# One-hot rows of a retrieval layer, built per token instead of per eight tokens

## The reference

```python
def _peer(h, w_query, sub_keys, expert_u, expert_v):
    ...                      # for each token and each of 8 heads: 16 picks
    eid = i1 * N_KEYS + i2   # i1, i2 in 0..127; 16384 experts
    g = jax.nn.softmax(best_s, axis=-1)
    ...
    a = jax.nn.gelu(jnp.einsum('td,thkd->thk', hx, expert_u[e]))
    return jnp.einsum('thk,thkd->td', gw * a, expert_v[e])
```

## Time and profile before

| | us |
|---|---|
| median of 3 runs | 1741.33 |
| profiled execution, its own time | 1739.58 |
| its span, first to last instruction | 1737.5 |
| PE busy | 1523.0 |
| DVE busy | 1347.0 |
| POOL busy | 967.2 |
| ACT busy | 384.0 |

### The profile page before, as it was taken

One profiled execution on the slowest core, in us unless ns is written; L12 is line 12 of the kernel. 1 busy time (PEld: TensorE's weight loads), 2 busy tenths in 40 slices (PEclk: granted clock), 3 DMA queues, 4 the chain that ended last, 5 costly groups with the idle time before them and its releaser, 6 DMA issues.

```text
span 1737.5 us, 17042 instructions
## 1 busy us (share of the span) xinstructions
PE 1523.0 (88%) x6242; PEld 949.3 (55%) x6242; DVE 1347.0 (78%) x1915; ACT 384.0 (22%) x834; POOL 967.2 (56%) x591
## 2 busy tenths in 40 slices
PE   9999999999979915888788887899989899999976
PEld 8988999988668802333233333445535544444432
DVE  6666656666797999767768888888868998788787
ACT  5665455564201212011010101020210101000000
POOL 3210000000364677887786776788888478788661
PEclk9999999999989957999999998999999889999998
DMA  9876443466799999999999999999999899999996
GB/s 322 286 258 218 121 146 122 139 203 241 273 382 419 379 425 425 411 425 426 425 424 424 417 422 419 422 414 423 424 420 426 346 380 411 410 404 406 425 427 273
DMA packets 159380, 615.39 MB, mean 354 GB/s; under 512 B 20915, under 2 KB 74255, under 8 KB 96703
## 3 DMA queue, kind: packets, MB, share of 16 engines
q0 software_dynamic: 79232, 485.32, 68.1%
q1 hardware_dynamic: 80064, 128.99, 20.7%
HBM read 683.42 MB, written 2.10 MB: 395 GB/s over the span
## 4 chain that ended last, share of the span: by engine, by line
PE 29%; POOL 21%; DMA 18%; DVE 16%; issue 13%; DVEq 2%; ACT 1%; SPq 0%; POOLq 0%; ACTq 0%
PE psum_all L592 13%; DMA v_slot<-in_expert_v_dram,eid 12%; POOL v_slot L547 11%; POOL u_slot L528 9%; DVE u_slot L1793 8%; DMA u_slot<-in_expert_u_dram,eid 5%; PE psum_all L732 4%; PE psum_all L987 3%; DVE xh L1828 2%; PE psum_all L757 1%; PE psum_all L713 1%; PE psum_all L619 1%; PE psum_all L617 1%; POOL v_slot L550 1%; DMA wq_ring<-in_w_query_dram 0%
## 5 line engine op out<-in xcount | busy, mean ns | idle before, releaser
L1793 DVE SCALAR_TENSOR_TENSOR u_slot<-u_slot,xh 128x2048 f32<-128x2048 f32 x256 | 577.8, 2289 | 130.2 <-DMA u_slot<-in_expert_u_dram,eid 128.5
L987 PE MATMUL psum_all<-v_slot,diag 128*128 128x512 f32 x1152 | 556.1, 635 | 138.8 <-DMA v_slot<-in_expert_v_dram,eid 93.4
L528 POOL DMA_INDIRECT u_slot<-in_expert_u_dram,eid x256 | 452.6, 1768 | 290.1 <-DVE u_slot L1793 117.5
L547 POOL DMA_INDIRECT v_slot<-in_expert_v_dram,eid x224 | 420.8, 1879 | 92.7 <-issue 64.6
L987 PEld LDWEIGHTS psum_all<-v_slot,diag 128*128 128x128 f32 x1152 | 223.8, 201 | 448.2 <-issue 249.5
L1828 DVE SCALAR_TENSOR_TENSOR xh<-v_slot,gate,xh 128x2048 f32<-128x2048 f32 x100 | 235.2, 2352 | 52.2 <-DMA v_slot<-in_expert_v_dram,eid 45.4
L1411 DVE TENSOR_TENSOR w_lo<-w_ring,w_hi 128x512 fp32r<-128x512 f32 x240 | 156.8, 689 | 78.8 <-ACT w_hi L1036 75.6
L592 PE MATMUL psum_all<-act_hi,w_hi 128*128 128x256 f32 x640 | 184.6, 289 | 1.1 <-DVE w_lo L1411 1.0
L592 PE MATMUL psum_all<-act_hi,w_lo 128*128 128x256 f32 x640 | 180.7, 282 | 0.0
L592 PE MATMUL psum_all<-act_lo,w_hi 128*128 128x256 f32 x640 | 180.6, 282 | 0.0
L1036 ACT ACTIVATE w_hi<-w_ring 128x512 fp32r<-128x512 f32 x240 | 139.4, 622 | 42.8 <-PE psum_all L592 40.8
(11 more groups left out here) (293 smaller groups left out, 1608.4 us busy)
## 6 DMA issues: line engine op xcount, KB each, us to landing
w_ring<-in_w_in_dram SPq DMA_DIRECT2D x88, 512.0 KB, 4.8
u_slot<-in_expert_v_dram SPq DMA_DIRECT2D x40, 1024.0 KB, 8.9
wo_ring<-in_w_out_dram SPq DMA_DIRECT2D x32, 512.0 KB, 4.9
wq_ring<-in_w_query_dram SPq DMA_DIRECT2D x32, 512.0 KB, 10.1
w_ring<-in_cmp_k_w_dram POOLq DMA_DIRECT2D x16, 512.0 KB, 5.5
w_ring<-in_cmp_v_w_dram POOLq DMA_DIRECT2D x16, 512.0 KB, 4.3
u_slot<-in_expert_u_dram,eid POOLq DMA_INDIRECT x256
v_slot<-in_expert_v_dram,eid POOLq DMA_INDIRECT x256
```

Of the source, the lines that this page charges most:

```text
L528: nc.gpsimd.indirect_dma_start(out=u_slot[m % RU][:, :], out_offset=None, in_=expert_u[0], in_offset=bass.IndirectOffsetOnAxis(ap=eid[:, n ...
L547: nc.gpsimd.indirect_dma_start(out=v_slot[m % RV][:, :], out_offset=None, in_=expert_v[0], in_offset=src, bounds_check=ROWS - 1, oob_is_er ...
L987: ins = nc.tensor.matmul(bank[(4 if n < PH else 0) + q][:, :], diag[:, n % 2, k, :], v_slot[m % RV][:, 512 * q:512 * q + 512], start=(m in ...
L1793: V.scalar_tensor_tensor(u_slot[m % RU][:, :], u_slot[m % RU][:, :], 1.0, xh[:, n // PH, :], ALU.mult, ALU.mult, accum_out=u_dot[:, n, k:k ...
```

## The change

In `hot_rows` three operations on all eight tokens become two for each token. The comparison of the second key, 128 columns, takes the key as a per-partition scalar. The comparison of the first key, 40 columns, takes the key and the coefficient as two per-partition scalars, with the comparison and the product in one operation. The drain between goes, and the semaphore is raised by the last operation as before.

```diff
         def hot_rows(t, b):
 
             g, n = NG_T * t + b, PICKS[t]
-            cols = slice(G_TOK * b, G_TOK * b + G_TOK)
             if b == 0:
                 dve.wait_ge(S["pick_ok"], t + 1)
             if g >= 2:
                 dve.wait_ge(S["dense_mm"], g - 1)
-            row, key, coef = (pickT[0:n, t, i, cols].unsqueeze(2) for i in range(3))
-            V.tensor_tensor(hot1[0:n, g % 2, :, :], iota_row[0:n, :].unsqueeze(1).to_broadcast([n, G_TOK, FD]),
-                            row.to_broadcast([n, G_TOK, FD]), ALU.is_equal)
-            V.tensor_tensor(hot2[0:n, g % 2, :, :], iota_key[0:n, :].unsqueeze(1).to_broadcast([n, G_TOK, NKEY]),
-                            key.to_broadcast([n, G_TOK, NKEY]), ALU.is_equal)
-            dve.drain()
-            V.tensor_tensor(hot1[0:n, g % 2, :, :], hot1[0:n, g % 2, :, :], coef.to_broadcast([n, G_TOK, FD]), ALU.mult
-                            ).then_inc(S["hot_ok"], 1)
+            for i in range(G_TOK):
+                row, key, coef = (pickT[0:n, t, a, G_TOK * b + i:G_TOK * b + i + 1] for a in range(3))
+                V.tensor_scalar(hot2[0:n, g % 2, i, :], iota_key[0:n, :], key, None, ALU.is_equal)
+                ins = V.tensor_scalar(hot1[0:n, g % 2, i, :], iota_row[0:n, :], row, coef, ALU.is_equal, ALU.mult)
+            ins.then_inc(S["hot_ok"], 1)
```

## The result

The changed kernel takes **1751.88 us** (median of 4 runs, 1749.9 to 1753.85), the kernel before 1741.06 in the same comparison. The ratio is 1.0067, 95% interval 1.0053 to 1.0082: slower by 10.8 us, by the interval between 9 and 14. The forecast was 1753, range 1743 to 1769. The profiled execution took 1751.51 us with a span of 1749.5, 12.0 longer than before.

A forecast was written before the change was run, and what follows sets the result against it. DVE was taken to set the pace at the end of the dots (1358 to 1405 us), starving the DMA engines. The profiled 1739.58 us plus 1 + 11 makes 1751.6, and 1.75 to the median gives 1753 us, range 1743 to 1769.

The forecast's parts named there:

- The price of a call: One `hot_rows` call on DVE: 3.26 us instead of 2.10, a loss of 1.16 us, 37.1 us over 32 calls.
- half rate: In the new small DVE operations: f32 elements in SBUF go two at a time, 0.13 us for 256 elements.
- fixed part: In each new small DVE operation: 0.07 us start to start, 1.12 us a call for the 16 operations.
- the second scalar: In the 40-element DVE operations: not free, 0.12 us taken for two scalars; were it free, a call takes 2.78 us.
- First set: The 16 calls for tile 0: 18.6 us more DVE time against 21.9 us of waits; cost 1 us, 0 to 5.
- Second set: The 16 calls for tile 1: 18.6 us more, about 7 of 9.3 us of waits used, dots end 11 us later.
- the sum 1 + 11: Both sets of calls together: the end of the kernel moves by +12 us.
- Gaps are not refilled: Transfer gaps before 1405 us stay lost: a microsecond DVE loses at the dots' end moves the end by about one.
- Shared ports: Small DVE operations and POOL gathers hold each other up: up to 0.95 us more a call, 1768 us; chance 0.12.
- No half rate: The new DVE operations run without half rate: +1.86 us a call, +22 us, 1763 us; chance 0.10.
- Hidden: Dots end late but the row additions catch up by their waits: time stays at 1741 us; chance 0.08.
- Faster: Scalars load under the operation before: a call takes 1.8 us, 0.3 less, time 1736.5 us; chance 0.06.

The follow-up runs named there:

- e5: Changed kernel with the coefficient as a constant 0.5, so that no operation has two per-partition scalars; 1744.86 us against 1740.87 for the kernel before.
- e2: Kernel before with the new form only in the 16 `hot_rows` calls for tile 0, the early set; 1740.27 us against 1740.86.
- e1: Kernel before with the new form only in the 16 `hot_rows` calls for tile 1, the late set; 1749.43 us against 1740.86.
- e9: Kernel before with POOL's last 11 u gathers alternating with seven v gathers instead of all standing ahead of them; 1751.49 us against 1740.86.
- e3: Changed kernel with keys and coefficient as constants in the instructions, no per-partition scalars; 1741.67 us against 1740.86 for the kernel before.
- e7: Kernel before with the product with the coefficient moved from DVE to ACT for tile 1; 1743.81 us against 1740.87.
- e4: Kernel before with the 1024-element comparison done twice in each call, 1.14 us more DVE time in one long operation; 1752.48 us against 1740.86.
- e6: Kernel before with five extra 2048-element products and drains on DVE between the last dot and the row additions; 1747.35 us against 1740.87.
- e12: Kernel before with only three v gathers moved ahead of the last u gathers in POOL's list; 1743.46 us against 1740.86.

## Why the prediction was right

- **The price of a call.** 3.26 us forecast, 3.26 measured. Each term was met in a run of its own: half rate and fixed part (0.14 and 0.09 us without scalars, 0.137 and 0.091 forecast), 0.06 for the first scalar and 0.06 for the second (e5 against the changed kernel). The step with the least behind it was the second scalar. ACT's rows showed only that two are not free there, 183 ns for both; that on DVE the second costs as much as the first was assumed and came out, which is luck. It decided between +4 and +10.8 us. Over all calls DVE's busy time grew by 37.3 us, 37.1 forecast.
- **First set.** Waits were to hide it at a cost of 1 us, 0 to 5. e2 measures -0.6 us, from -3.1 to +0.5 by its interval. I had feared a late PE; it did not show.
- **Second set.** 11 us forecast of 18.6, with 7 of 9.3 us of waits used up. The changed kernel used 6.4 of them, its stretch to the last dot grew by 11.3 us, and e1 alone costs 8.6 us. Together with e2 that makes 8.0 of the 10.8 us; the rest is within the three intervals. Both terms of the sum 1 + 11 were thus a little high, by the medians.
- **Gaps are not refilled.** The conclusion held, one microsecond at the last dot for about one at the end, and the DMA share fell as said; the same 157 MB took 388 and 401 us. The reason was too simple. e9 filled part of the gap before 1405 us and it came back behind it, so it is not the bytes moved before the last dot that count, but all the idle time of the DMA engines up to the end of the additions. Why that time cannot be filled is shown for the v gathers alone, which wait for their seven slots until the additions begin (34.4 us in e9). That the first dense loads too wait for DVE, for the u slots of its dots, is argued from the order of the lists. And nothing was won the other way: in their profiled executions e3 and e7 had the last dot 2.5 us earlier, and their medians did not fall.
- **The rivals.** Shared ports: e4 gives the same time with none of the small operations, so they add nothing measurable here. No half rate: the 0.14 us of e3 rule it out. Hidden: not at the end of the dots, but for tile 0; behind the last dot a small part may be (e6, open). Faster: the scalars are not loaded under the operation before; even without them (e3) nothing is gained.
- **Luck in the sum.** The profiled execution of the changed kernel was 2.0 us late before the first changed instruction; runs of one kernel differ by that much (the kernel before 1738.73 to 1745.38 us over the 17 runs beside e9 to e12). The agreement to 1.1 us is better than the method.

## What to carry to other kernels

Price many small DVE operations by their starts, not their durations: here 0.07 us each, 0.06 for every per-partition scalar, and only then the elements. A broadcast operation over all eight tokens that reads its key as a second tensor pays the 0.07 once and no scalar. Then look at where the calls stand: the same 18.6 us cost nothing where DVE waited for gathers and some 9 us where it set the pace. And test the other direction before moving work away: an engine whose loss shows at the end can have nothing to win.

## What the runs showed of the hardware

- **Two per-partition scalars on DVE are paid one after the other**, 0.06 us each from start to start, also with both ALU steps in one operation.
- **A gather on POOL that starts during a dot ends 0.9 us behind it.** In the kernel before 16 of the 35 gathers between 1302 and 1405 us start in a dot. Fifteen end 0.9 to 1.0 us behind that dot, or behind the next one where it follows at once; the last (1396.25 us, 10.24 us long) is held over four dots and the scaling of `xh`. One that starts elsewhere takes 0.94 to 1.3 us. In the changed kernel 10 of 35 start in a dot, and the others take 0.94 to 1.1 us. POOL's u gathers by line (ns min/median/max): the kernel before from 1302 to 1405 us, then the changed kernel from 1302 to 1418, then e4 from 1302 to 1405:

```profile
L528 POOL DMA_INDIRECT u_slot<-in_expert_u_dram,eid x21: 942/2020/3002, 1302.6 to 1379.5; - x21
```
```profile
L528 POOL DMA_INDIRECT u_slot<-in_expert_u_dram,eid x21: 943/982/2760, 1303.3 to 1388.2; - x21
```
```profile
L528 POOL DMA_INDIRECT u_slot<-in_expert_u_dram,eid x20: 1182/2642/5807, 1301.4 to 1384.6; - x20
```

  With the same DVE time in long operations (e4) the median rises from 2020 to 2642 ns, in small ones it falls to 982, and the two kernels take the same time. So the durations of the gathers do not set it here. That the small size of the operations alone does this is not shown: in e3, with small operations and short calls, 15 of 35 gathers are held by a dot, about as many as before.
- **A gather stretches a small operation at its own end, mostly without moving the next.** The second kind by line, the last of one call and the dot behind it, then the gather beside them, in the changed kernel:

```profile
L1817 DVE TENSOR_SCALAR hot<-iota_row,pickT x256: 284/293/542, 1116.1 to 1408.7; 128x40 f32<-128x40 f32 x64, 96x40 f32<-96x40 f32 x64
...
1390.04 0.53 DVE L1817 TENSOR_SCALAR hot<-iota_row,pickT 96x40 f32<-96x40 f32 x1
1390.25 2.28 DVE L1793 SCALAR_TENSOR_TENSOR u_slot<-u_slot,xh 128x2048 f32<-128x2048 f32 x1
...
1389.49 1.09 POOL L547 DMA_INDIRECT v_slot<-in_expert_v_dram,eid  x1 [0.30 <-issue]
```

  0.53 us instead of 0.29: the operation ends at 1390.57 us, the gather at 1390.58, and the dot still starts 0.21 behind. Where the starts were 0.09 apart (e3, 1371.11 us) one such meeting moved the following start by some 0.13 us. The Trainium skill ("SBUF — State Buffer", section "Who interferes with whom") has it that of a 2-port VectorE operation and a GpSimd one the second is blocked for the whole of the first. The trace does not agree for small operations behind a gather: three of them and the dot start within the gather of 1389.49 us at the usual 0.20 to 0.21 us, and the hold is about 0.25 us at most.
